# Re-ordering the entry of the first mixer: key weights ahead of constants, two rows between modulation blocks, gate sums behind the first key projection

## The reference, cut to what matters

```
mod   = silu(c)     @ w_ada + b_ada            # 6*1024 numbers: sh1, sc1, g1, ...
mod_c = silu(c_ctx) @ w_ada + b_ada
hc = rms_norm(ctx, norm1_gain) * (1 + csc1) + csh1
hx = rms_norm(x,   norm1_gain) * (1 + sc1)  + sh1
rq, rk, rv, rg, mq, mk, mv, mo, mg, bg_ret, bg_ml = (h @ w for w in split(w_in))   # for hc and hx
# mg: 16 gate columns; log_sigmoid, cumulative sums and a running maximum over time
# ctx side: per-token weights times keys, then states = keys^T @ values
# x side: retention and mLSTM started from these states
```

## Time and profile before

| | |
|---|---|
| median of 3 runs | 1945.36 us (1942.80 to 1948.59) |
| the profiled execution's own time | 1945.66 us |
| its span in the trace | 1943.9 us |
| PE busy | 1720.1 us (88%) |
| DVE, ACT, POOL busy | 628.3 (32%), 328.4 (17%), 74.4 (4%) |
| mean granted TensorE clock | 0.96 of full speed |
| DMA | 582.38 MB, mean 300 GB/s |

### The profile page before, as it was taken

The page is one execution under the profiler, slowest core; times in us unless marked ns, Lnnn a source line. Parts: engine busy times, 40 slices in busy tenths (PEclk is TensorE's granted clock), DMA queues, the critical chain, the costliest instruction groups (busy, mean ns, idle before and its releaser), DMA issues.

```text
span 1943.9 us, 23833 instructions
## 1 busy us (share of the span) xinstructions
PE 1720.1 (88%) x10280; PEld 1072.5 (55%) x10280; DVE 628.3 (32%) x1323; ACT 328.4 (17%) x690; POOL 74.4 (4%) x82
## 2 busy tenths in 40 slices
PE   7999999999999999999988888889999766565787
PEld 4557688888888545463333332247677333232355
DVE  3896155587832156141111111133133000010002
ACT  3302240100101244031111100022242100000001
POOL 0001121000000000000000000000140000000000
PEclk8999999999999999999999999999999878787899
DMA  9789325777653032169999999992435999999996
GB/s 399 279 355 390 121 99 204 275 288 299 253 227 130 1 156 110 49 242 411 428 428 427 428 428 427 428 424 105 168 127 208 426 429 426 428 427 428 426 428 251
DMA packets 43881, 582.38 MB, mean 300 GB/s; under 512 B 4864, under 2 KB 5248, under 8 KB 7936
## 3 DMA queue, kind: packets, MB, share of 16 engines
q1 hardware_dynamic: 43776, 580.85, 72.6%
HBM read 579.78 MB, written 1.05 MB: 299 GB/s over the span
## 4 chain that ended last, share of the span: by engine, by line
PE 56%; DMA 35%; DVE 6%; ACT 1%; issue 1%; SPq 0%; DVEq 0%; POOL 0%; ACTq 0%
PE banks L679 35%; DMA ring<-in_experts_dram 33%; PE banks L1263 7%; PE banks L1305 3%; PE banks L1144 3%; DMA ring<-in_weights_dram 2%; DVE ring L2038 2%; PE banks L961 1%; PE banks L664 1%; PE banks L1007 1%; DVE small L2468 1%; PE banks L600 1%; PE banks L1118 1%; PE banks L1030 1%; PE banks L614 0%
## 5 line engine op out<-in xcount | busy, mean ns | idle before, releaser
L1263 PE MATMUL banks<-ring,arena 128*32 128x256 f32 (+1 forms) x2944 | 375.7, 510 | 135.4 <-DMA ring<-in_experts_dram 135.4
L679 PE MATMUL banks<-hT,ring 128*128 128x256 f32 (+1 forms) x1744 | 398.1, 390 | 8.4 <-ACT hT L1600 7.1
L679 PEld LDWEIGHTS banks<-hT,ring 128*128 128x128 f32 x1744 | 333.2, 192 | 71.8 <-issue 29.0
L1263 PEld LDWEIGHTS banks<-ring,arena 128*32 128x32 f32 (+1 forms) x2944 | 140.3, 132 | 352.1 <-issue 193.0
L2038 DVE SCALAR_TENSOR_TENSOR ring<-ring 128x1024 f32<-128x1024 f32 x192 | 237.6, 1237 | 9.5 <-DMA ring<-in_weights_dram 0.7
L1305 PE MATMUL banks<-ring,arena 128*32 128x256 f32 (+1 forms) x1536 | 187.4, 488 | 40.9 <-DMA ring<-in_experts_dram 39.2
L2678 DVE TENSOR_TENSOR arena<-arena,banks 128x512 f32<-128x512 f32 (+1 forms) x32 | 17.7, 554 | 508.8 <-PE banks L1263 508.8
L679 PE MATMUL banks<-arena,ring 128*128 128x256 f32 (+2 forms) x720 | 150.5, 371 | 3.7 <-POOL arena L2805 1.6
L1305 PEld LDWEIGHTS banks<-ring,arena 128*32 128x32 f32 (+1 forms) x1536 | 70.5, 126 | 143.5 <-issue 88.7
L679 PE MATMUL banks<-ring,hT 128*128 128x512 f32 (+1 forms) x384 | 145.9, 540 | 0.6 <-DMA ring<-in_weights_dram 0.6
L679 PEld LDWEIGHTS banks<-arena,ring 128*128 128x128 f32 (+1 forms) x720 | 131.1, 189 | 23.2 <-POOL arena L2805 2.0
(11 more groups left out here) (332 smaller groups left out, 1256.7 us busy)
## 6 DMA issues: line engine op xcount, KB each, us to landing
ring<-in_experts_dram SPq DMA_DIRECT2D x185, 2048.0 KB, 30.5
ring<-in_weights_dram SPq DMA_DIRECT2D x73, 2048.0 KB, 10.1
ring<-in_weights_dram SPq DMA_DIRECT2D x8, 1408.0 KB, 6.3
arena<-in_experts_dram SPq DMA_DIRECT2D x2, 2048.0 KB, 8.3
ring<-in_experts_dram SPq DMA_DIRECT2D x8, 512.0 KB, 29.7
ring<-in_weights_dram SPq DMA_DIRECT2D x2, 1152.0 KB, 26.2
cT<-in_ctx_dram SPq DMA_DIRECT2D x2, 1024.0 KB, 9.1
ring<-in_weights_dram SPq DMA_DIRECT2D x2, 1024.0 KB, 19.4
```

What stands on the lines that cost most here:

```text
L679: ins = mm(dst, a, b, start=(i == 0), stop=(i == len(terms) - 1))
L1263: ins = mm(banks[M * q:M * q + M, which, 0:W], xc[:, 4 * half + k, :], w[k][:, W * q:W * q + W], start=(half == 0 and k == 0), stop=(half ...
```

## The change

Six things move; nothing is computed differently.

1. SP issues rk directly behind a3, and `phase` and the gate weights behind rk.
2. PE makes `sil_row(2)` behind the rows of a1 and `sil_row(3)` behind the rows of a2; DVE copies them behind its bias sums of a0 and a1.
3. `affine` gives ACT the even features and DVE the odd ones, and each instruction raises the flag.
4. `c_rk0` starts feature by feature behind these flags.
5. The gate sums (16 + 2 matmuls of L707 and L714) stand behind `c_rk0`, and wait for all eight features of both streams.
6. The turned columns stand between the context and the sequence jobs of rv; before, they stood behind all of rk. On DVE, `ctx_keys(0, ·)` stands behind `source_rows`, ahead of `gate_rows(0, 1)`; before, it stood behind `mod_sum` of a4.

```diff
@@ PE
             for b in range(4):
                 mods("a", b)
+                if b in (1, 2):
+                    sil_row(b + 1)
             mods_end()
-            for v in (2, 3):
-                sil_row(v)
-            eng.wait_ge(flag("gate_weights_in"), 16)
-            ...
+            def first_gates():
+                eng.wait_ge(flag("gate_weights_in"), 16)
+                for s in (1, 0):
+                    eng.wait_ge(flag(f"h1_{s}"), 4)
+                    eng.wait_ge(flag(f"h1_{s}_v"), 4)
+                    ...
                     o = jobs.bank(job)
-                    project(token_major(o, 1, c, w)).then_inc(*jobs.fills(job))
-                for c in range(TC):
-                    job = f"x_{n}{c}"
-                    ...
-                if n == "rk":
+                    project(token_major(o, 1, c, w),
+                            first=["h1_1"] if n == "rk" and c == 0 else []).then_inc(*jobs.fills(job))
+                    if n == "rk" and c == 0:
+                        first_gates()
+                if n == "rv":
                     eng.wait_ge(flag("source_rows"), 1)
                     ...
+                for c in range(TC):
+                    job = f"x_{n}{c}"
+                    ...
@@ SP
-            for name in names[:4]:
+            for name in names[:5]:
                 load(name)
             eng.dma_start(phase[:], t["const_ret"]).then_inc(flag("ret_consts_in"), 16)
             eng.dma_start(carve(G0 + 2944, 384), t["gates"]).then_inc(flag("gate_weights_in"), 16)
-            for name in names[4:]:
+            for name in names[5:]:
@@ ACT
-                for k in range(KD // 2):
-                    ins = A(hT[:, s, k, :], hT[:, s, k, :], ACT.Identity, scale=gainA[:, s, k:k + 1],
-                            bias=shift_of(L, which, c, k))
-                ins.then_inc(*act.raises(hname))
+                for k in range(0, KD, 2):
+                    A(hT[:, s, k, :], hT[:, s, k, :], ACT.Identity, scale=gainA[:, s, k:k + 1],
+                      bias=shift_of(L, which, c, k)).then_inc(*act.raises(hname))
@@ DVE
-                for k in range(KD // 2, KD):
+                for k in range(1, KD, 2):
                     ...
             for b in range(4):
                 mod_evac("a", b)
+                if b in (0, 1):
+                    sil_rows_copied(b + 2)
             ...
-            for v in (2, 3):
-                sil_rows_copied(v)
             ...
             raise_after("source_rows")
+            ...
+            for c in range(TC):
+                ctx_keys(0, c)
             gate_rows(0, 1)
             ...
             raise_after("mc_rep")
-            ...
-            for c in range(TC):
-                ctx_keys(0, c)
             for b in (5, 6, 7, 8, 9, 10, 11):
                 mod_sum("a", b)
```

More of the change, by code:

```diff
@@ L692, in _ @@
                 mods("a", b)
+                if b in (1, 2):
+                    sil_row(b + 1)
             mods_end()
-            for v in (2, 3):
-                sil_row(v)
-            eng.wait_ge(flag("gate_weights_in"), 16)
[L698 to L715, removed]
+            def first_gates():
[3 more added lines that the diff above has]
+                    eng.wait_ge(flag(f"h1_{s}_v"), 4)
+                    if jobs.new(f"gate_parts{s}") > 1:
+                        eng.wait_ge(*jobs.is_free(f"gate_parts{s}"))
+                    o = jobs.bank(f"gate_parts{s}")
+                    for r in range(2):
+                        for g in range(4):
+                            k = 2 * g + r
+                            ins = mm(o[32 * g:32 * g + 32, 0:N], mg_w[:, k, :], hT[:, s, k, :],
+                                     start=(r == 0), stop=(r == 1), skip_group_check=True)
+                    ins.then_inc(*jobs.fills(f"gate_parts{s}"))
+                for s in (1, 0):
+                    eng.wait_ge(*jobs.is_drained(f"gate_parts{s}"))
+                    if jobs.new(f"gates{s}") > 1:
+                        eng.wait_ge(*jobs.is_free(f"gates{s}"))
+                    mm(jobs.bank(f"gates{s}")[:, 0:N], mg_spread, mg_part[s],
+                       start=True, stop=True).then_inc(*jobs.fills(f"gates{s}"))
@@ L753, in _ @@
                     mm(o[:, 0:64], mc[0:64, :].broadcast_to((64, P)), ident[0:64, 0:64], start=True, stop=True).then_inc(*jobs.fills("mc_rep"))
+                for c in range(TC):
+                    job = f"x_{n}{c}"
+                    if jobs.new(job) > 1:
+                        eng.wait_ge(*jobs.is_free(job))
+                    o = jobs.bank(job)
+                    if n[1] == "v":
+                        project(token_major(o, 0, c, w)).then_inc(*jobs.fills(job))
+                    else:
+                        project([(o[:, N * j:N * j + N],
+                                          [(w[:, k, P * (2 * c + j):P * (2 * c + j) + P], hlat[:, k, :])
+                                           for k in range(KD)]) for j in range(2)]).then_inc(*jobs.fills(job))
+                used(n, job)
             for n in ("c_rk1", "c_rv1"):
@@ L2082, in affine @@
                 eng.wait_ge(*dve.last)
-                for k in range(KD // 2, KD):
-                    ins = TS(hT[:, s, k, :], hT[:, s, k, :], gainA[:, s, k:k + 1], shift_of(L, which, c, k),
-                             ALU.mult, ALU.add)
-                ins.then_inc(*dve.raises(hname))
+                for k in range(1, KD, 2):
+                    TS(hT[:, s, k, :], hT[:, s, k, :], gainA[:, s, k:k + 1], shift_of(L, which, c, k),
+                       ALU.mult, ALU.add).then_inc(*dve.raises(hname))
             def scale_shift(tag, s, src, L, which, hname):
@@ L2208, in _, with ctx_keys @@
             raise_after("source_rows")
+            def ctx_keys(m, c):
+                job = f"c_{('rk', 'mk')[m]}{c}"
+                eng.wait_ge(*jobs.is_filled(job))
+                o = jobs.bank(job)
+                for d in range(2):
+                    w = src_ret[:, d, c, :] if m == 0 else wcols[:, c, 32 * d:32 * d + 4]
+                    ins = TT(k_src[m][d][:, c, :].rearrange("p (h n) -> p h n", h=HEADS),
+                             o[:, :].rearrange("p (h n) -> p h n", h=HEADS), columns(w, P), ALU.mult)
+                ins.then_inc(*dve.frees(job))
+            for c in range(TC):
+                ctx_keys(0, c)
             gate_rows(0, 1)
```

## The result

| | before | after |
|---|---|---|
| median | 1945.09 us (1941.51 to 1949.89, 19 runs) | 1949.43 us (1947.44 to 1951.76, 19 runs) |
| profiled execution: own time, span | 1945.66, 1943.9 us | 1949.94, 1948.1 us |
| mean granted TensorE clock | 0.96 | 0.959 |

The ratio of after to before is 1.0024, 95% interval 1.0016 to 1.0032: 4.3 us slower. 2.4 us were forecast, with up to 1.7 more for one short fall of the clock near the start of rk, and that fall came.

What follows compares the result with a forecast made beforehand. PE behind mv sets the end one for one, with DVE's block sums as second path through mk. Terms +1.3 (mk), -0.56 (mv), +1.7 (clock) gave +2.4 us: 1947.8 us on the median's scale, range 1943 to 1953.

Steps and rivals of the forecast that it cites:

- short fall of the clock: One fall of the granted clock between 31 and 40 us, costing at most 1.7 us, giving 1949.8; inside the forecast.
- PE's front: From a1's rows to rk: full clock, rk starting at 36.3 us, 8.5 us sooner; gate sums return 3.2.
- DVE's path: Block sums up to a6: gate parts 1.6 us late, ctx_keys adding 2.55, turned columns awaited, a6 summed at 92.9.
- mk: Load issued after a6's sum, landing 9.2 us later at 102.1; PE waits 6.5 us, mk starts 1.3 later.
- The clock behind that wait: Behind PE's wait for mk the granted clock falls, costing 1.7 us of PE time; nearby bounds 0 and 3.4.
- mv: Behind mk's matmuls, mv no longer waits, so the 0.56 us of PE idle time ahead of it goes.
- The kept gain: Rival at mk: it lands by 95.6 us and PE keeps 5.3 us, 1940.4; chance 0.04 including anything else ahead.
- the order of loads: Rival at the front: rk lands at 38.5 us as before and starts 2.2 us later, 1950.3 us; chance 0.06.
- mk was not quick: Denies the rival that mk lands at 100.7 us and the clock holds, 1945.0 us; chance 0.15.
- The half clock from the start: Rival at the front: half clock behind 25.35 us, a3's rows 5.3 to 6.9 later, 1953 to 1955 us; chance 0.13.

Runs made afterwards that it cites:

- e2: The changed kernel with DVE's sums of a4 and a5 split into its logarithm waits and a6 summed ahead of the columns' copies: 1941.45 us, ratio 0.9975.
- e4: The changed kernel with the two sil rows back behind a3's columns, on PE and DVE: 1951.95 us, ratio 1.0032.
- e7: The changed kernel with the turned columns back behind all of rk: 1948.67 us, one execution.
- e1: The changed kernel with DVE's copies of the turned columns behind the sums of a4, a5 and a6: 1948.57 us, one execution.
- e6: e2 with sil_row(3) behind a3's columns instead of behind a2's rows: 1944.56 us, ratio 0.9993.
- e5: The kernel before with the sums of a4 and a5 in DVE's waits and a6's sum ahead of ctx_keys: 1949.25 us, ratio 1.0024.

## Why the prediction was right, and where its sizes were off

- **PE's front.** Right: rk forecast at 36.3, found at 36.30. The gate sums end at 46.96, forecast 45.4. The difference is the first key job, 8.80 us where the sum had 6.95, less 0.2 that the gate sums took less. The prediction named a short fall of the clock between 31 and 40 us, at most 1.7 us, and left it out of the sum; it was 1.85. All later positions carry it.
- **DVE's path.** Right in each link, and late by that one term: `source_rows` 61.97 (60.4), start of a4's sum 75.01 (73.4), DVE stopped by the turned columns (0.76 us), start of a5's sum 83.88 (82.3), a6 summed 94.44 (92.9). Every link is 1.5 to 1.6 us behind the forecast. The changes of place cost what they were said to cost. One part of this was luck: the prediction took a4's sum at 7.1 us as before, and put one instruction of 2.17 us into it. Before, a second one was hit as well (the bias sum, 1.10 us where it takes 0.16 alone); in after other instructions were hit, again two, and the sum took 7.1 us once more.
- **mk.** Forecast 9.2 us from issue to landing, found 9.36; PE's wait forecast 6.5, found 6.62; mk starts 3.0 us later than before (forecast 1.3, the same 1.6 on top, and mk's 0.16). The estimate of 6.8 us from the Trainium skill (DMA: Bandwidth & Descriptors, "Anatomy of one DMA") is not borne out for this transfer; the row was the better guide.
- **The clock behind that wait.** Forecast 1.7 us from a stretch some 265 us further on, found 16.10 - 13.90 = 2.2. The rule of the Trainium skill (TensorE: Matmul & The Clock Gate, "Why this matters for your kernels") that idle time takes the matmul engine back to its lower rate is what this trace shows: 0.82, then 0.50, through 6.6 us without matmuls and 4 us beyond.
- **mv.** Right: its 0.56 us went. Sum by the rows of after: 3.0 + 2.2 - 0.56 = 4.6, the shift of mv's start; span +4.2, medians +4.3.
- **Rivals.** The kept gain was priced at 1940.4 and called almost excluded in this order. It did not come in this order, and with a6's sum out of the way (e2) the time is 1941.45. rk's first matmul waited for ACT's feature and not for its weights, so the order of loads did what was said, and mk was not quick. The half clock from the start did not come; e4, which is near to it, costs 6.65 us where the rival had 7.3 and more.

The step that failed is a size: the first key job's clock belonged in the sum, since PE's idle stretch ahead of it (1.57 us behind tiny columns, and 0.72 before) looks like others behind which the trace of before showed a fall.

What stays open is when that fall comes. The same order of instructions gave a first key job of 7.11 (e7), 8.80 (after, e2) and 10.17 us (e1) with the same idle stretch ahead of it. An idle stretch of 1.2 us behind the columns does not decide it either: ahead of a3's rows the clock fell behind one (e6 and e5), and ahead of a2's rows it did not (e4 and e5, granted clock 1.00 to 30 us).

## What to carry to other kernels

A front that gets an engine to work sooner is worth what the next load allows: follow the slot back to its last reader, and that reader's whole queue, before pricing it. Here the matmul engine came 3.6 us sooner to a block whose issue had moved 4 us the other way, and moving most of two sums into DVE's waits, and a third ahead of the copies of the columns, turned a loss of 4.3 us into a gain of 3.9. The same move on the kernel before was worth nothing, or cost 4.8 us where it delayed the freeing of a bank: price an edit on the kernel it will stand in.

## What the runs showed of the hardware

POOL and DVE meet twice in each of these kernels. POOL of after, and two DVE instructions beside it:

```profile
76.01 1.36 POOL L2789 TENSOR_TENSOR arena<-arena,phase 128x512 f32<-128x512 f32 x1 [72.07 <-ACT arena L1670]
77.85 1.72 POOL L2789 TENSOR_TENSOR arena<-arena,phase 128x512 f32<-128x512 f32 x1 [0.48 <-ACT arena L1670]
```

```profile
76.28 2.16 DVE L2041 SCALAR_TENSOR_TENSOR ring<-ring 128x1024 f32<-128x1024 f32 x1
...
78.49 2.17 DVE L2041 SCALAR_TENSOR_TENSOR ring<-ring 128x1024 f32<-128x1024 f32 x1
```

The second meeting in before:

```profile
74.44 1.94 POOL L2787 TENSOR_TENSOR arena<-arena,phase 128x512 f32<-128x512 f32 x1 [2.80 <-ACT arena L1667]
```

```profile
75.29 1.10 DVE L2044 TENSOR_TENSOR mod<-mod,vec 128x4 f32<-128x4 f32 x1
```

Each DVE instruction with two inputs in SBUF, the on-chip memory, that starts while a POOL instruction runs is 0.94 to 1.02 us longer (2.16 and 2.17 against 1.22), and one that had started before it is not. In the trace of before the second one hit was a bias sum of four columns, 1.10 us where it takes 0.16 alone. So the price went with the meeting and not with the DVE instruction's size, and before and after paid it twice each. What sets it can be read from the 22 meetings of the eleven traces: POOL's instruction ends 1.07 to 1.16 us behind the start of the DVE instruction that it holds up. Where a DVE instruction was under way when POOL's started, POOL's ends 1.11 to 1.14 us behind the end of that one, whatever its own length (1.28 to 1.99 us). So the two take turns: POOL waits out the DVE instruction under way, and the next DVE instruction waits out POOL's. The Trainium skill (GPSIMD Engine Reference, "Specifications") names the shared memory interface for DVE instructions with two such inputs, which these are.

The first fall of the clock is not the same from one execution to the next in one order of instructions (7.11, 8.80, 8.80, 10.17 us for the first key job), so a single trace does not tell its mean price.
